# Expert weights loaded in release order, and three smaller edits, in a two-layer decoder trunk with 64 experts

## The reference, cut to what matters

```
g_sel = argmax(x @ router_group)               # 1 group of 4
top_p, top_i = top_k(softmax(e_logits), 2)     # 2 experts of its 8
y = (silu(xb @ w1[e]) * (xb @ w3[e])) @ w2[e]  # for the tokens of e
x = x + sum of gates * y                       # then the next layer
```

## Time and profile before

| what | us |
|---|---|
| three runs | 1755.37, 1750.96, 1745.83 |
| median | 1750.96 |
| the profiled execution's own time | 1747.62 |
| its span | 1745.9 |

### The profile page before, as it was taken

One profiled execution on the slowest core, in us unless ns is written; L12 is line 12 of the kernel. 1 busy time (PEld: TensorE's weight loads), 2 busy tenths in 40 slices (PEclk: granted clock), 3 DMA queues, 4 the chain that ended last, 5 costly groups with the idle time before them and its releaser, 6 DMA issues. The chain is left out here.

```text
span 1745.9 us, 27516 instructions
## 1 busy us (share of the span) xinstructions
PE 1632.2 (93%) x11158; PEld 875.4 (50%) x11287; DVE 977.9 (56%) x1657; ACT 459.5 (26%) x777; POOL 157.0 (9%) x188
## 2 busy tenths in 40 slices
PE   7999877889899999999998999999899999999996
PEld 6756666655533333333334977665533333333333
DVE  4548566581336666676666322561336666666666
ACT  4353444372311111111112321462211111111112
POOL 2002524310100000000000040120100000000000
PEclk9999999999999999999999999999999999999998
DMA  6441000028599999999996250208699999999993
GB/s 200 115 127 55 7 3 4 5 96 307 230 370 425 426 425 425 427 425 424 426 422 229 77 193 24 97 2 332 227 384 425 427 424 425 426 426 425 425 421 160
DMA packets 102256, 475.40 MB, mean 272 GB/s; under 512 B 28913, under 2 KB 67825, under 8 KB 76528
## 3 DMA queue, kind: packets, MB, share of 16 engines
q1 hardware_dynamic: 98752, 461.03, 65.5%
q0 software_dynamic: 3376, 12.58, 1.9%
HBM read 454.71 MB, written 18.87 MB: 271 GB/s over the span
## 5 line engine op out<-in xcount | busy, mean ns | idle before, releaser
L723 PE MATMUL ps<-w_unit,xT 128*48 128x512 f32 x1024 | 451.9, 594 | 3.8 <-DVE xT L780 3.0
L724 PE MATMUL ps<-w_unit,xT 128*48 128x512 f32 x1024 | 452.0, 594 | 0.0
L820 DVE SCALAR_TENSOR_TENSOR x<-ps,gate_by_expert,x 128x512 f32<-128x512 f32 x512 | 348.3, 744 | 178.2 <-PE ps L775 178.1
L723 PEld LDWEIGHTS ps<-w_unit,xT 128*48 128x48 f32 x1024 | 125.9, 123 | 308.9 <-issue 305.5
L753 PE MATMUL ps<-w_unit,hidT 128*48 128x512 f32 x1024 | 247.2, 603 | 12.1 <-issue 12.1
L775 PE MATMUL ps<-y_high_low,slots_to_tokens 128*128 128x512 f32 x512 | 154.3, 422 | 8.1 <-DVE y_high_low L795 5.2
L843 ACT ACTIVATE y_high_low<-ps 48x512 fp32r<-48x512 f32 x128 | 75.8, 592 | 322.1 <-PE ps L753 320.5
L775 PEld LDWEIGHTS ps<-y_high_low,slots_to_tokens 128*128 128x128 f32 x512 | 86.1, 188 | 123.2 <-DVE x L820 57.0
L1294 PE MATMUL ps<-hT_high,w_high 128*128 128x512 f32 (+1 forms) x336 | 135.5, 403 | 7.1 <-PE ps L1296 4.0
L836 ACT ACTIVATE gate_act_hid<-ps 48x512 f32<-48x512 f32 x64 | 37.9, 593 | 372.3 <-PE ps L724 372.3
L1296 PE MATMUL ps<-hT_high,w_low 128*128 128x512 f32 (+1 forms) x336 | 133.0, 396 | 0.0
(11 more groups left out here) (368 smaller groups left out, 1972.2 us busy)
## 6 DMA issues: line engine op xcount, KB each, us to landing
w_unit<-in_moe_w SPq DMA_DIRECT2D x184, 2048.0 KB, 28.3
w_unit<-in_moe_w SPq DMA_DIRECT2D x16, 1024.0 KB, 33.0
x_rows<-sorted_rows SPq DMA_DIRECT2D x64, 192.0 KB, 26.5
w_unit<-in_od_w_qkv SPq DMA_DIRECT2D x12, 1024.0 KB, 5.5
w_raw<-in_ev_w_in SPq DMA_DIRECT2D x10, 1024.0 KB, 6.1
sorted_rows<-bias SPq DMA_DIRECT2D x32, 192.0 KB, 5.6
w_unit<-in_ev_w_out SPq DMA_DIRECT2D x2, 2048.0 KB, 10.6
w_unit<-in_od_w_out SPq DMA_DIRECT2D x2, 2048.0 KB, 11.3
```

Of the source, the lines that this page charges most:

```text
L723: nc.tensor.matmul(ps_1[0:MB, :], xT[b][:, k, :], w1[:, k, :], start=k == 0, stop=k == KD - 1)
L724: last = nc.tensor.matmul(ps_3[UP:UP + MB, :], xT[b][:, k, :], w3[:, k, :], start=k == 0, stop=k == KD - 1)
L820: nc.vector.scalar_tensor_tensor(out=xs, in0=ps_c[i % 4][:, :], scalar=gate(t), in1=xs, op0=ALU.mult, op1=ALU.add).then_inc(added, 1)
```

## The change

- **Router:** buffer 8 is loaded when 7 of the 8 output tiles are projected (its half of the weights has then been used), and buffer 9's wait for the eighth is written ahead of it.
- **Release order:** `place` no longer counts modulo 11; a new piece takes the buffer that is released next by PE's program.
- **`OWN` = 31:** the down products lag one expert up to expert 30, whose own come after its up products and down(29); only expert 31 does its own.
- **Early halves:** the first four reloaded pieces, (3,2), (4,0), (4,1), (4,2), come in halves of 1 MB, the first two halves at the middle of up(0) (`up_half`), and so on. The tokens of expert 1 are turned in the middle of up(0). The up products of expert 0 write bank 4 in place of bank 3, so up(1) need not wait for hid(0).
- **Next stage's loads** wait for the last user of each guest buffer singly.
- **Chunks:** the key Gram moves behind update(1); DVE does up to two search rounds ahead of its masks.
- **Sparse:** the add over both heads and the maximum over both become one `tensor_tensor_reduce` for each head, with the sign turned; ACT waits for each head singly.

```diff
-            sp.wait_ge(out_done, 2 * TT)
+            sp.wait_ge(out_done, 2 * TT - 1)
             wts.load(sp, GUEST[:1])
...
+            sp.wait_ge(out_done, 2 * TT)
             wts.load(sp, GUEST[1:])
...
+LAST, OWN = N_EXP - 1, N_EXP - 1
+def in_order_of_release():
+    pieces = [(0, 0), (0, 1)]
+    for n in range(1, OWN):
+        pieces += [(n, 0), (n, 1), (n - 1, 2)]
+    pieces += [(OWN - 1, 2)]
+    for n in range(OWN, N_EXP):
+        pieces += [(n, 0), (n, 1), (n, 2)]
+    return pieces
+def places():
+    released, where, uses = in_order_of_release(), {}, [0] * UNITS
+    for p in range(N_EXP * len(PARTS)):
+        j = p if p < UNITS else where[released[p - UNITS]][0]
+        where[divmod(p, len(PARTS))] = j, uses[j]
+        uses[j] += 1
+    return released, where, uses
...
-    LAST, OWN = N_EXP - 1, 19
...
+            if isinstance(n, int) and n < len(EARLY) // 2 and k == KD // 2 - 1:
+                last.then_inc(up_half, 1)
...
+            def load_early(gone):
+                for half_, done in enumerate((up_half, up_done)):
+                    sp.wait_ge(done, gone + 1)
+                    for piece in EARLY[2 * gone:2 * gone + 2]:
+                        wts.load_half(sp, *piece, half_)
...
                     squares(lv)
-                    if lv == 1:
-                        gram((B[2], B[3]), ka, both, False, 2 * CH)
                     if lv > 1:
                         update(lv - 1)
+                    if lv == 2:
+                        gram((B[2], B[3]), ka, both, False, 2 * CH)
...
-                    V_.tensor_tensor(lg[i % DEEP][:, :, 0:L], ps_z[i % 2][:, :, 0:L], bias,
-                                     ALU.add).then_inc(biased, 1)
-                    dve.wait_ge(biased, i + 1)
-                    V_.tensor_reduce(nmax[:, i, :], lg[i % DEEP][:, :, 0:L], AX.X, ALU.max,
-                                     negate=True).then_inc(maxed, 1)
+                    for a in range(2):
+                        V_.tensor_tensor_reduce(out=lg[i % DEEP][:, a, 0:L], in0=ps_z[i % 2][:, a, 0:L],
+                                                in1=m.bias[:, t, 0:L], scale=-1.0, scalar=-4.0 * NEG, op0=ALU.add,
+                                                op1=ALU.min, accum_out=nmax[:, i, a:a + 1]).then_inc(maxed, 1)
```

More of the change, by code:

```diff
@@ L590 @@
 EXTRA = (0, 1, 2)
+LAST, OWN = N_EXP - 1, N_EXP - 1
[14 more added lines that the diff above has]
+    return released, where, uses
+RELEASED, PLACES, LOADS = places()
 def place(n, part):
-    use, j = divmod(len(PARTS) * n + part, UNITS)
-    return j, use
+    return PLACES[n, part]
 HALVED = (N_EXP - 2, N_EXP - 1)
-LOADS = [sum(place(n, part)[0] == j for n in range(N_EXP) for part in range(len(PARTS))) for j in range(UNITS)]
+EARLY = [divmod(p, len(PARTS)) for p in range(UNITS, UNITS + 4)]
+IN_HALVES = EARLY + [(n, part) for n in HALVED for part in range(2)]
 class ExpertWeights:
@@ L610, in __init__ @@
         self.landed = [c.lasting_sem(f"unit_in{j}") for j in range(UNITS)]
-        self.rest_landed = [[c.lasting_sem(f"rest_in{n}_{part}") for part in range(2)] for n in HALVED]
+        self.rest_landed = {piece: c.lasting_sem(f"rest_in{piece[0]}_{piece[1]}") for piece in IN_HALVES}
     def start_layer(self, w1, w3, w2):
@@ L638, in load_half @@
         eng.dma_start(self.view(n, part)[:, rows, :], expert(self.dram[part], n, 2 * k)[:, rows, :]).then_inc(
-            self.rest_landed[HALVED.index(n)][part] if half else self.landed[place(n, part)[0]], 16)
+            self.rest_landed[n, part] if half else self.landed[place(n, part)[0]], 16)
     def arrived(self, pe, n, part):
@@ L644, in arrived @@
         pe.wait_ge(self.landed[j], 16 * (use + 1))
+        if (n, part) in EARLY:
+            pe.wait_ge(self.rest_landed[n, part], 16)
     def load_guest(self, eng, w_dram):
@@ L657, in end_layer @@
     def end_layer(self, c):
-        c.of_stage += self.landed + [s for pair in self.rest_landed for s in pair]
+        c.of_stage += self.landed + list(self.rest_landed.values())
         self.__init__(c)
@@ L834, in silu @@
     def silu(act, n):
+        if isinstance(n, int) and n == 1:
+            act.wait_ge(hid_done, n)
         act.wait_ge(up_done, n + 1)
-        nc.scalar.activation(gate_act, ps_1[0:MB, :], ACT.Silu).then_inc(silu_done, 1)
+        nc.scalar.activation(gate_act, ps_up(n)[0:MB, :], ACT.Silu).then_inc(silu_done, 1)
     def split_high(act, n):
@@ L865, in freed @@
             def freed(n, part):
-                gone, was = divmod(len(PARTS) * n + part - UNITS, len(PARTS))
+                gone, was = RELEASED[len(PARTS) * n + part - UNITS]
                 sp.wait_ge(down_done if was == 2 else up_done, gone + 1)
+            def load_early(gone):
[3 more added lines that the diff above has]
+                        wts.load_half(sp, *piece, half_)
             for n in range(SLOTS, N_EXP):
@@ L887, in _ @@
                 users = [max(n for n in range(N_EXP) for part in range(len(PARTS)) if place(n, part)[0] == j) for j in GUEST]
-                sp.wait_ge(down_done, max(users) + 1)
-                ahead.load(sp, [wts.unit[j] for j in GUEST])
+                ahead.load(sp, [wts.unit[j] for j in GUEST], lambda i: sp.wait_ge(down_done, users[i] + 1))
             def more(e, b, m):
@@ L905, in _ @@
             up_expert(pe, 0, -1)
-            turn_rows(pe, 1, 0)
             for n in range(1, OWN):
@@ L1204, in __init__, with load @@
         self.raw_in = [c.lasting_sem(f"w_raw_in{i}") for i in range(self.N)]
-    def load(self, sp, guest):
+    def load(self, sp, guest, free):
         halves = [tile[:, h * KD * GC:(h + 1) * KD * GC] for tile in guest for h in range(2)]
@@ L2628, in _ @@
                 B[3].empty(V_.tensor_tensor(QbT[half(1), 1, :, :], gram[1][half(0), :, CH:P], masks(3, half(0)), ALU.mult))
+                before, between, behind, last = ROUNDS[t]
+                search.rounds(dve, min(2, before))
                 for par in range(2):
@@ L2631, in _ @@
                     B[2 + par].empty(V_.tensor_tensor(NQ[:, par, :, :, :], o, later, ALU.mult))
-                before, between, behind, last = ROUNDS[t]
-                search.rounds(dve, before)
+                search.rounds(dve, before - min(2, before))
                 if t:
```

36 lines of the change are left out of this document (22 added, 14 removed).

## The result

The changed kernel took 1752.03 us (median of 20 runs) against 1747.7 us (20 runs), ratio 1.0026 (95% 1.0015 to 1.0036): by the ratio 4.5 us slower (2.6 to 6.3), where 3 us faster was forecast. The time lies inside the forecast's wide range of 1733 to 1757, but the change went the other way. Its profiled execution has a span of 1750.0 us against 1745.9.

What follows compares the result with a forecast made beforehand. Expert stages were taken as bound by weight DMA (15.3 us per expert against PE's 13.99), both arriving together at the end. Chunks -6, sparse attention -4, experts with router +7 gave -3: 1748.0 us against the median, range 1733 to 1757.

Steps and rivals of the forecast that it cites:

- the chunks: Mixer's chunk tiles: moving the key Gram removes PE's waits for DVE; -6 us, between -7.7 and -3.
- Sparse attention: Mixer's sparse part: merged add and maximum take 1.5 us per unit instead of 2.44; -4 us, between -6 and +3.
- may grow: Chunk tiles: PE's later pauses without any releaser, up to 2 us, could grow and reduce the gain.
- its own sign of being wrong: Chunk tiles: the forecast is wrong if they keep their 33 us per tile.
- (c): Expert stage's end: 37.4 us from (29,1)'s landing to up(31), including 9.44 us from the last hidden transposition to up(31).
- (a): Expert stage's start: DMA gaps filled, gaining 4.4 and 4.0 us; 420 or more GB/s in each window from 482.
- (b): Expert stages: up(1)'s gain of 1.50 us is hidden; PE waits for weights from about expert 22, some 10 us per layer.
- Rival 2: Expert stages: early halves don't bring (29,1) forward, longer tail is paid, +8.4 and +7.0 us; 1756.4 us; chance 0.08.
- (d): Router: buffer 8's earlier load slows tile 1's scatter, ACT's square of tile 3 starts 2.0 us late; net +0.2 and +0.3.
- rival 4: Sparse attention: the merged operation is two passes, so its gain is about 0; 1752 us; chance 0.08.
- Rival 1: Expert stages: PE's pace alone counts, the lag pays, up(31) 6.9 us earlier in both layers; 1727 us; chance 0.17.
- rival 3: Router: tile 1's scatter lands before 463.2, gaining 1.9 us twice; 1744 us; chance 0.10.

Runs made afterwards that it cites:

- experiment 7: Changed kernel (lag to expert 31) with the four early pieces loaded whole instead of in halves; ratio 1.0053 to the kernel before.
- experiment 3: Changed kernel with 40 small unused matmuls keeping PE busy in the pause before it catches up near up(31); ratio 1.003 to the kernel before.
- experiment 1: Changed kernel with the lag ending at expert 19 again, all other edits kept; ratio 0.9969 to the kernel before.
- experiment 2: Changed kernel with the lag ending at expert 25; ratio 0.9995 to the kernel before.
- experiment 8: Kernel before with only the lag to expert 31 added, own piece order and whole loads; ratio 1.0095, 16.6 us.
- experiment 12: Changed kernel with lag to 20, small matmuls in the turn, and 12 more behind the odd mixer's projection; ratio 0.9938 to the kernel before.

## Why the prediction was wrong

Stage lengths between marks in the traces, in us, medians over all profiles that share the code. Chunks: from their first Gram to the first product of the sparse attention. Sparse attention: to the end of its last product, 2.3 us ahead of the router's first instruction. Router: from there to the first token rows. up(31): from those.
```
                         unchanged code (profiles)    changed code (profiles)   change   forecast
chunks                   132.2  (4; 130.2 to 132.8)    130.2  (10; 128.1 to 133.0)  -2.0     -6
sparse attention          47.5  (3; 47.5 to 48.3)       43.8  (11; 43.8 to 45.8)    -3.8     -4
router, layer 0           80.6  (6; 80.4 to 81.2)       81.6  (8; 80.8 to 82.1)     +1.0     +0.2
router, layer 1           80.0  (6; 79.7 to 80.4)       78.7  (8; 77.8 to 81.2)     -1.3     +0.3
up(31), layer 0          450.2  (4; 449.9 to 451.9)    456.3  (2, with 7)           +6.1     +3.8
up(31), layer 1          450.1  (4; 448.0 to 451.0)    453.9  (1, changed)          +3.8     +2.7
sum                                                                                 +3.8     -3
```
The sum agrees with the 4.5 us measured (2.6 to 6.3). In the last row experiment 7 had 456.7. **The step that failed is the chunks**: the term "I take -6 (between -7.7 and -3)" measured -2 by the profiles and +0.7 (-1.7 to +3.1) by the times of the kernel with that edit alone. That is 4 to 7 us, the larger part of the miss. The first half of the mechanism ran as told. In tile 1 the squares of the third level started at 252.61, which with the 2.78 us by which the tile began earlier is 255.4 against the forecast 255.7 and 258.54. What failed is that I ended the reckoning there. PE in tile 1 after:
```profile
251.73 1.08 PE L2448 MATMUL ps<-kk_r,k 64*64 64x128 f32 x32
252.61 0.45 PE L2420 MATMUL ps<-A,AT 64*64 64x64 f32 x17
...
257.67 0.82 PE L2420 MATMUL ps<-AT,A 64*64 64x64 f32 x24 [0.81 <-issue]
258.25 1.10 PE L2420 MATMUL ps<-XT,A_eye 64*64 64x64 f32 x32
...
263.51 0.69 PE L2420 MATMUL ps<-XT,A_eye 64*64 64x64 f32 x32 [1.20 <-POOL A_eye L2390]
```
The half clock moved from the Gram (1.99 us for 32 in the earlier trace rows, 1.08 here) to the products at 258.25 (1.10 us for what takes 0.65 at full clock; granted clock 0.50 in 258 to 261), and PE now waits 1.2 us for POOL, which was 0.18 us in the kernel before:
```profile
267.95 0.69 PE L2374 MATMUL ps<-XT,A_eye 64*64 64x64 f32 x32 [0.18 <-POOL A_eye L2344]
```
At these products 263.51 + 2.78 = 266.3 stands against 267.95: of the 3.1 us gained at the third level (258.54 against 255.4) 1.7 are left. Over all four tiles, waits of PE before, then after:
```profile
PE ps L2374 <- issue: 8.7, 12, 2.1
PE ps L2402 <- DVE QbT L2628: 6.3, 4, 1.8
...
PE ps L2374 <- ACT AT L2542: 2.4, 6, 0.5
...
PE ps L2374 <- POOL A_eye L2344: 0.6, 2, 0.4
```
```profile
PE ps L2420 <- issue: 10.2, 14, 1.5
PE ps L2420 <- ACT AT L2588: 3.6, 5, 0.8
...
PE ps L2420 <- POOL A_eye L2390: 1.6, 2, 1.2
```
The wait of 6.3 us is gone and 1.5 + 1.2 + 1.0 = 3.7 us of it stand under other names. The prediction named this danger (pauses "may grow") and gave it less than it took; its own sign of being wrong, chunks that keep 33 us per tile, is nearly what came (132.2 / 4 = 33.0, now 32.6).

**The second mis-sized term is the turn in (c), taken at its rare row.** 9.44 us came from the earlier trace rows, a turn at full clock; the turn of layer 1 in the same trace took 10.7, and I left it aside. By experiment 3's count the short one is 2 cases in 18. It took 11.8 and 10.8 us here, 3.7 more than the two 9.44. With this the experts cost 9.9 us where 6.5 were forecast. With the lag at 19 the same loss stood in most profiles too, but ahead of up(29), where in the prediction's own reckoning PE had a little slack; at 31 nothing covers it.

**Point by point, the rest.**

(a) Right but for a few GB/s: 410 to 435 in each window of 4 us from 482 to 542, where 420 or more was asked; up(29) at 416.4 us where 899.1 - 4.4 + 0.2 - 478.45 = 416.45 was forecast, in layer 1 414.9. But most is due to the order of release, of which I had said that it "brings nothing more", and not to the halves: by experiment 7 these gave nothing in layer 0 and 1.6 us in layer 1. I cost the halved loads at nothing. The Trainium skill, DMA: Bandwidth & Descriptors (anatomy of one DMA), has a fixed 2.0 us for each DMA on the GpSimd path; taken serially for these loads of SP that would be, as an estimate, 8 us a layer. The trace does not show such a cost: with and without halves up(29) of layer 0 stands at 416.4 and 416.3, so whatever is fixed in a DMA overlaps here.

(b) Right: waits for weights of 11.3 and 9.8 us, forecast "some 10", from expert 20 (forecast 22).

(c) Direction right, 37.4 us forecast between the landing and up(31), 40.0 and 39.0 measured; experiments 1, 2 and 8 show it from three sides. Rival 2 named this mechanism ("the longer tail is paid") as the way to be slower; its other condition, that (29,1) does not come forward, did not hold.

(d) ACT, POOL and the landing in layer 0 after:
```profile
455.58 1.06 ACT L443 ACTIVATE xn<-x 128x1024 f32<-128x1024 f32 x1 [8.41 <-DMA sorted_rows<-xn,dest]
```
```profile
446.25 0.96 POOL L579 DMA_INDIRECT sorted_rows<-xn,dest  x1 [0.30 <-issue]
...
464.20 0.96 POOL L579 DMA_INDIRECT sorted_rows<-xn,dest  x1 [0.30 <-issue]
```
Tile 1's scatter took 455.58 - 446.25 = 9.3 us beside the load (forecast 9.1), and the square of tile 3 came 2.2 us late for it (465.4 in the time of the kernel before, against 463.18). The last scatter, without a load beside it, took 5.7 us in layer 0, not the 4.4 I had given it. Over the profiles it took 5.3 us (median) against 6.4, 1.1 less, which with the 2.2 gives the +1.0. In layer 1 the square came late too (67.0 us behind the router's start against 65.1). Its last scatter took 3.6 us in all eight profiles with the early load, but the router 77.8 to 81.2 us, in the changed kernel itself 80.9; so the -1.3 of the medians is not explained. In the sum the two are next to nothing.

**Sparse attention**: right by the profiles (-3.8), while the times of the kernel with that edit alone show 1.9 us (4.0 at most). The merged operation, durations min/median/max in ns:
```profile
L2799 DVE CUSTOM_DVE_ANT_0 prob<-ps,bias x32: 285/488/692, 343.4 to 382.3; 128x512 f32<-128x512 f32 x8, 128x384 f32<-128x384 f32 x8, 128x256 f32<-128x256 f32 x8, 128x128 f32<-128x128 f32 x8
L2799 DVE DVE_READ_ACCUMULATOR2_ANT minus_max<- x32: 82/83/84, 344.0 to 382.5; 128x1 f32 x32
```
692 + 83 ns for 512 columns, 1.55 us a unit where 1.5 was forecast. That is no more than DVE's other two-input operation on 128x512 (744 ns in the earlier trace rows), so it is no two passes, and rival 4 is out. Rival 1 (the lag pays) is out by experiments 2 and 8, rival 3 by the wait of ACT for the scatter, in both layers.

One reading of the two single traces was wrong too: that the mixer had given its full 10 us. What stands ahead of the chunks, which no edit touches, ended (at the first Gram) 213.1 to 218.6 us from the span's start in the 14 profiles, 2.4 us earlier in the changed kernel's than in that of before; and the chunks of before were near the long end of theirs. What a pair of single profiles differ by is not yet an edit's worth.

## What to carry to other kernels

When one resource sets the pace and another the work behind its last delivery, place the catching up where the first still gives slack: here at expert 19 or 20, where PE is about to wait, not at 25 and not at 31 (19 and 20 were not compared with all else equal). A wait that goes is worth what the end of its whole chain gains, so follow it to the last instruction of the stage and ask which engine is late next. Give the length of a step behind an idle stretch of PE at half clock too, with the chance of it, or fill the stretch. And look for a second case of the row that a term is sized by: here layer 1 of the same trace had it.

## What the runs showed of the hardware

The same pause of PE costs or does not. Timeline of PE at the start of the odd mixer's attention, code that no edit touches, before and then after, and windows of the same stretches (PEclk third from the end):
```profile
1105.38 1.99 PE L1442 MATMUL ps<-kT,qT 64*128 64x512 f32 x8 [1.97 <-PEq L78]
...
1106.00:1110.00 4.00, 4.00 (x40) 2.17 (x37) 1.67 (x3) 2.62 (x4) 1.45 (x2) 1.00 0.81 272
```
```profile
1103.35 2.83 PE L1488 MATMUL ps<-kT,qT 64*128 64x512 f32 x8 [2.01 <-PEq L78]
...
1104.00:1108.00 4.00, 4.00 (x28) 2.29 (x25) 1.70 (x2) 2.64 (x3) 0.81 (x2) 0.57 0.87 284
```
A pause of 2.0 us with the same work around it leaves TensorE at 2.4 GHz once (granted clock 1.00) and at 1.2 GHz for most of the next 4 us the other time (0.57). In the 13 profiles with this pause the part from this row to the router's first product takes 75.2 us in 5 and 76.8 in 8, with no regard to the kernel; experiment 12, with 1.4 us, took 75.2. The longer pause of the turn, 2.61 us, was followed by the low clock in 16 of 18 cases, and shortened to 0.3 us in none of 10. The Trainium skill, TensorE: Matmul & The Clock Gate (part 1, the clock gate), says that the activity monitor's window runs freely and does not start with the kernel; the rows fit that, in that the same pause has both outcomes. Such a loss belongs into a forecast with its chance, not with the one outcome that a single trace shows.
